# x loaded last, the last three blocks of w_ada summed on VectorE, and a new order of the Gram, index and corner steps

## The reference

```python
mod = c @ w_ada + b_ada                       # c (1, 1024), w_ada (1024, 3072)
shift, scale, gate = split(mod, 3)
h = rmsnorm(x, pre_norm_gain) * (1 + scale) + shift
proj = h @ w_in                               # 10,328 columns
# branch A: an indexer picks 128 keys per query, then softmax attention
logits = einsum('bqhd,bsd->bqhs', rope(q_idx), rope(k_idx)) * 64 ** -0.5
score = einsum('bqh,bqhs->bqs', w_idx, relu(logits)) * 8 ** -0.5
# branch B: gated delta rule in chunks, 8 heads
lower = where(strict, einsum(kb, kc) * decay, 0)   # the Gram product of the keys
t_mat = inverse(lower + eye)
u, w = t_mat @ vb, t_mat @ (kb * exp(gc)); then a scan over the chunks
y = sigmoid(ga) * y_a + sigmoid(gb) * y_b
out = x + gate * rmsnorm(y @ w_o, post_norm_gain)
```

## Time and profile before

| | |
|---|---|
| median of 3 runs | 853.12 us (852.45 to 854.57) |
| profiled execution | 849.76 us, its span 848.0 us, mean TensorE clock 0.989 |
| TensorE matmuls busy | 812.6 us, 96% |
| VectorE / GpSimd / ScalarE busy | 439.2 / 394.3 / 332.2 us |
| moved by DMA | 95.63 MB |

### The profile page before, as it was taken

One profiled execution on the slowest core, in us unless ns is written; L12 is line 12 of the kernel. 1 busy time (PEld: TensorE's weight loads), 2 busy tenths in 40 slices (PEclk: granted clock), 3 DMA queues, 4 the chain that ended last, 5 costly groups with the idle time before them and its releaser, 6 DMA issues.

```text
span 848.0 us, 11222 instructions
## 1 busy us (share of the span) xinstructions
PE 812.6 (96%) x4070; PEld 653.4 (77%) x4070; DVE 439.2 (52%) x953; ACT 332.2 (39%) x702; POOL 394.3 (46%) x335
## 2 busy tenths in 40 slices
...
GB/s 311 344 58 145 142 187 184 110 106 100 69 118 93 91 92 102 74 102 82 81 58 92 51 75 74 76 75 75 74 75 75 75 174 125 196 151 75 199 27 100
DMA packets 166801, 95.63 MB, mean 113 GB/s; under 512 B 35009, under 2 KB 158274, under 8 KB 165722
## 3 DMA queue, kind: packets, MB, share of 16 engines
...
...
## 4 chain that ended last, share of the span: by engine, by line
PE 73%; DVE 11%; DMA 5%; ACT 4%; SPq 3%; issue 2%; POOL 1%; POOLq 0%; DVEq 0%; ACTq 0%
PE ps L685 17%; PE ps L687 17%; PE ps L686 16%; PE ps L956 2%; PE ps L1007 2%; PE ps L1006 2%; PE ps L1005 2%; DMA w_ada_sb<-in_w_ada 2%; PE ps L943 2%; PE ps L796 2%; PE ps L724 2%; ACT prob L1258 2%; DVE kraw L1699 1%; DVE prob L1879 1%; PE ps L950 1%
## 5 line engine op out<-in xcount | busy, mean ns | idle before, releaser
L1356 POOL TENSOR_TENSOR w_lo<-raw,w_hi 128x512 fp32r<-128x512 f32 (+1 forms) x218 | 297.4, 1387 | 327.0 <-ACT w_hi L1029 310.8
L685 PE MATMUL ps<-h_hi,w_hi 128*128 128x512 f32 (+1 forms) x680 | 291.3, 428 | 3.2 <-ACT xT L1051 1.1
L687 PE MATMUL ps<-h_hi,w_lo 128*128 128x512 f32 (+1 forms) x680 | 268.0, 394 | 0.0
L686 PE MATMUL ps<-h_lo,w_hi 128*128 128x512 f32 (+1 forms) x680 | 266.9, 393 | 0.0
L685 PEld LDWEIGHTS ps<-h_hi,w_hi 128*128 128x128 f32 (+1 forms) x680 | 128.9, 190 | 30.3 <-issue 5.0
L687 PEld LDWEIGHTS ps<-h_hi,w_lo 128*128 128x128 f32 (+1 forms) x680 | 128.3, 189 | 29.3
L686 PEld LDWEIGHTS ps<-h_lo,w_hi 128*128 128x128 f32 (+1 forms) x680 | 129.1, 190 | 25.2 <-issue 3.4
L1029 ACT ACTIVATE w_hi<-raw 128x1024 fp32r<-128x1024 f32 (+1 forms) x109 | 113.6, 1051 | 25.9 <-PE ps L1007 17.1
L1198 ACT ACTIVATE o_tok<-ps 128x128 f32<-128x128 f32 x32 | 8.9, 277 | 91.8 <-PE ps L908 91.7
L1006 PE MATMUL ps<-w_lo,y_hi 128*128 128x256 f32 x128 | 36.2, 283 | 0.0
L1007 PE MATMUL ps<-w_hi,y_lo 128*128 128x256 f32 x128 | 36.2, 283 | 0.0
...
## 6 DMA issues: line engine op xcount, KB each, us to landing
...
```

Source lines behind the costliest of these rows:

```text
L685: pe.matmul(out_ap, w_hi[:, slot, k, 0:m], rhs_hi(k), start=(k == 0), stop=False)
L686: pe.matmul(out_ap, w_hi[:, slot, k, 0:m], rhs_lo(k), start=False, stop=False)
L687: mm = pe.matmul(out_ap, w_lo[:, slot, k, 0:m], rhs_hi(k), start=False, stop=(k == KT - 1))
L1356: ins = pool.tensor_tensor(w_lo[:, slot, ks, 0:n], raw[:, slot, ks, 0:n], w_hi[:, slot, ks, 0:n].bitcast(F32), ALU.subtract)
```

## The change

Seven edits, all in the first third of the program:

- SyncE issues all eight w_ada blocks before x.
- TensorE multiplies blocks 0 to 4 as before. VectorE forms c5 * block 5 + c6 * block 6 + c7 * block 7 in place of block 5, and TensorE multiplies this with a matrix of ones. Three filler products follow.
- ScalarE makes the sine tables before the squares; GpSimd makes a root per x tile; VectorE scales tiles 0 and 1 before mod and tiles 2 and 3 behind the first `scales`.
- w_lo of unit 2 is made by VectorE behind the last h_lo, and GpSimd goes on with unit 3.
- Gram products 0 to 3 get a bank each (5, 4, 6, 7) and come one round earlier; Gram 5, 6 and 7 come later.
- The rotation of the index rows comes one round earlier on GpSimd and VectorE; they go back in two halves, the second behind the store of the inverse; ScalarE takes the index steps ahead of the key steps within a round.
- The first four heads' corners end at round 51 instead of 53, and the zeroing moves from rounds 22, 26, 40, 43 to 2, 10, 46, 50.

```diff
-R_GRAM = [12, 13, 14, 17, R_DELTA[0] + 1, R_DELTA[0] + 4, R_DELTA[0] + 7, R_DELTA[1] + 6]
+R_GRAM = [11, 12, 13, 16, R_DELTA[0] + 1, R_DELTA[0] + 6, R_DELTA[1] + 3, R_DELTA[1] + 7]
-R_PAIR = [[42, 44, 45, 47, 49, 50, 52, 53], ...
+R_PAIR = [[41, 42, 44, 45, 47, 48, 50, 51], ...
-    GRAM_BANK = [5, 4, 5, 4, 5, 5, 5, 5]
+    GRAM_BANK = [5, 4, 6, 7, 5, 5, 5, 5]
 # SyncE
-        conditioning(2)
-        conditioning(3)
+        for k in range(2, KT):
+            conditioning(k)
         for i in range(NT):
             sp.dma_start(x_sb[:, i, :], x[blk(i), :]).then_inc(s_x[i], 16)
-        for k in range(4, KT):
-            conditioning(k)
...
-            if r == R_TURN + 3:
-                index_rows_back()
+            if r == R_TURN + 2:
+                index_rows_back((0, 1))
...
                 if r == R_STORE[b]:
                     store_inverse(b)
+                    if b == 0:
+                        index_rows_back((2, 3))
...
-            if r in (22, 26, 40, 43):
-                clear(((22, 26, 40, 43).index(r),))
+            if r in (2, 10, 46, 50):
+                clear(((2, 10, 46, 50).index(r),))
 # TensorE
-        condition(range(2, KT)).then_inc(*pro_pe.inc("mod"))
+        condition(range(2, K_VEC))
+        pe.wait_ge(*pro_pool.at("ones"))
+        pe.wait_ge(*pro_dve.at(f"acc{KT - 1}"))
+        for n in range(4):
+            mm = pe.matmul(bank(2 + n), ones_p[:], w_ada_sb[:, K_VEC, n * S:(n + 1) * S], start=False, stop=True)
+        mm.then_inc(*pro_pe.inc("mod"))
+        for _ in range(3):
+            pe.matmul(bank(0), cb[:, KT - 1, :], w_ada_sb[:, KT - 1, 0:S], start=True, stop=True)
...
         def gram(h):
             pe.wait_ge(*key_dve.at("s", h))
-            if h >= 2:
-                pe.wait_ge(*gram_dve.at("L", h - 2 if h < 4 else h - 1))
+            if h == 2:
+                pe.wait_ge(*small_dve.at("gc"))
+                pe.wait_ge(*small_act.at("gcT"))
             if h >= 4:
-                pe.wait_ge(*solve_act.at("kd", h // 7))
+                pe.wait_ge(*gram_dve.at("L", h - 1))
+                pe.wait_ge(*solve_act.at("kd", h // 6))
 # ScalarE: the three sines move ahead of the four squares; index_rows(r) moves ahead of small(r)
 # GpSimd
+            pool.tensor_scalar(small_cols[:, 4 + i:5 + i], small_cols[:, i:i + 1], 1.0 / D, EPS, ALU.mult, ALU.add)...
+            pool.tensor_tensor(small_cols[:, 4 + i:5 + i], small_cols[:, 4 + i:5 + i], nhalf[:, 0:1], ALU.pow)...
-        pool.wait_ge(*pro_dve.at("lo7"))
-        for q in range(2, RING):
-            split(q)
+        pool.wait_ge(lo_made, 3)
+        split(3)
-            if r == R_TURN + 1:
+            if r == R_TURN:
                 index_rows()
 # VectorE
+        acc = w_ada_sb[:, K_VEC, :]
+        for k in range(K_VEC, KT):
+            c_col = pcol[:, 0, R_C + k:R_C + k + 1]
+            dve.wait_ge(s_ada[k], 16)
+            if k == K_VEC:
+                dve.tensor_scalar(acc, acc, c_col, None, ALU.mult)...
+            else:
+                dve.scalar_tensor_tensor(out=acc, in0=w_ada_sb[:, k, :], scalar=c_col, in1=acc, op0=ALU.mult, op1=ALU.add)...
...
+        scale_rows(0)
+        scale_rows(1)
         dve.wait_ge(*pro_pe.at("mod"))
...
         scales(0)
+        scale_rows(2)
+        scale_rows(3)
...
+        dve.tensor_tensor(w_lo[:, 2], raw[:, 2], w_hi[:, 2].bitcast(F32), ALU.subtract).then_inc(lo_made, 1)
```

More of the change, by code:

```diff
@@ L53 @@
 RING = 4
+K_VEC = 5
 PROJ_BANKS = 3
@@ L87 @@
 R_STORE = [R_INV[b] + len(INV_ROWS[b]) for b in range(2)]
-R_PAIR = [[42, 44, 45, 47, 49, 50, 52, 53], [R_DELTA[2] + n for n in (12, 14, 16, 18, 20, 24, 26, 27)]]
+R_PAIR = [[41, 42, 44, 45, 47, 48, 50, 51], [R_DELTA[2] + n for n in (12, 14, 16, 18, 20, 24, 26, 27)]]
 R_LOAD = [max(R_DELTA[h] - 2, R_PAIR[h // 4][-1] + 3) for h in range(HEADS)]
@@ L176, in program @@
     nhalf = place("nhalf", [P, 8])
+    ones_p = place("ones_p", [P, P])
     m8 = place("m8", [P, 3, 8])
@@ L364, in program @@
     pro_pe = steps("pro_pe", ["rowsT", "rows2T", "mod"] + [f"x{k}" for k in range(KT)])
-    pro_act = steps("pro_act", [f"ssq{i}" for i in range(NT)] + ["sinA", "sinI", "cos"]
+    pro_act = steps("pro_act", ["sinA", "sinI", "cos"] + [f"ssq{i}" for i in range(NT)]
                     + [f"{a}{k}" for n in range(0, KT, 2) for a, k in (("hi", n), ("h", n + 1), ("hi", n + 1))])
@@ L368, in program @@
                                 "wrap", "rc2", "clamp", "clampc", "pcol2", "hgain"]
-                    + [f"xn{i}" for i in range(NT)] + [f"{a}{k}" for k in range(4) for a in ("shift", "scale")] + ["mb0", "scg0"]
+                    + [f"acc{k}" for k in range(K_VEC, KT)] + ["xn0", "xn1"]
+                    + [f"{a}{k}" for k in range(4) for a in ("shift", "scale")] + ["mb0", "scg0", "xn2", "xn3"]
                     + ["h0", "lo0", "shift4", "scale4", "lo1", "shift5", "scale5", "h2", "lo2", "shift6", "scale6", "lo3",
                        "shift7", "scale7", "mb1", "scg1", "h4", "lo4", "lo5", "h6", "lo6", "lo7"])
-    pro_pool = steps("pro_pool", ["half", "ms", "rstd", "kpadE", "kpadO", "zero"])
+    pro_pool = steps("pro_pool", ["half", "ones"] + [f"{a}{i}" for i in range(NT) for a in ("ms", "rstd")] + ["kpadE", "kpadO", "zero"])
     small_pe = steps("small_pe", ["smT", "gc", "gl", "gcT", "kT"])
@@ L592, in index_rows, with index_rows_back @@
                 sp.dma_start(isw[32 * n + 16 * b:32 * n + 16 * b + 16, 0, :], iq[64 * b:64 * b + 16, n, :]).then_inc(s_turned, 16)
-        def index_rows_back():
+        def index_rows_back(pairs):
             sp.wait_ge(*iq_dve.at("ad"))
-            for n in range(4):
+            for n in pairs:
                 for b in range(2):
@@ L723, in condition @@
                 for n in range(4):
-                    mm = pe.matmul(bank(2 + n), cb[:, k, :], w_ada_sb[:, k, n * S:(n + 1) * S], start=(k == 0),
-                                   stop=(k == KT - 1))
-            return mm
+                    pe.matmul(bank(2 + n), cb[:, k, :], w_ada_sb[:, k, n * S:(n + 1) * S], start=(k == 0), stop=False)
         pe.wait_ge(*pro_dve.at("cb"))
@@ L1029, in split @@
             act.activation(w_hi[:, slot, :, 0:n], raw[:, slot, :, 0:n], ACT.Copy).then_inc(hi_made, 1)
+        act.wait_ge(s_cols, 16)
+        act.wait_ge(*pro_dve.at("clampc"))
+        for t, name in ((0, "sinA"), (1, "sinI")):
+            act.activation(tab_sin[:, t, :], rp[:, 2, t * S:(t + 1) * S], ACT.Sin, scale=cols[:, 2 + t:3 + t]).then_inc(
+                *pro_act.inc(name))
+        act.activation(tab_cos[:].rearrange("p a b -> p (a b)"), rp[:, 3, :], ACT.Sin).then_inc(*pro_act.inc("cos"))
         for i in range(NT):
@@ L1311, in _ @@
                 attend(h, r - R_ATT[h])
+            index_rows(r)
             small(r)
@@ L1325, in _ @@
                     up_decay(h)
-            index_rows(r)
             for n in range(KT):
@@ L1360, in _ @@
         pool.memset(nhalf[:], -0.5).then_inc(*pro_pool.inc("half"))
+        pool.memset(ones_p[:], 1.0).then_inc(*pro_pool.inc("ones"))
         pool.wait_ge(*pro_pool.at("half"))
```

32 lines of the change are left out of this document (16 added, 16 removed).

## The result

The changed kernel takes 831.75 us (median of 4 runs, 830.45 to 832.78) against 853.48 for the kernel before (4 runs, 852.45 to 854.57): a ratio of 0.974, with a 95% interval of 0.972 to 0.977, so 21.7 us less. The forecast was 839.0, with a range of 829 to 849. The direction and the range held; the gain was 7.6 us larger than forecast.

The account below looks back on a forecast made before the run. TensorE, busy 812.6 of 848.0 us, was taken as the bound, with its waits and slow clock to win. Terms 3.5 + 0 + 7.0 + 7.4 - 1.3 - 2.5 = 14.1 us, so 853.1 - 14.1 = 839.0, range 829 to 849.

Parts of the forecast that it names:

- prologue: Before the rounds: h of tile 0 starts at 37.9 to 38.0 against 41.5, 3.5 us won (1.8 to 3.8).
- Grams and index rows, by round 39: Up to round 39: earlier L of head 3 and index rows, less a new relu wait, win 7.0 us (4.0 to 11.2).
- corners, U, Gram 5: Around 160 to 200 us: earlier corners and U, later Gram 5; 7.4 us won after Gram 6's 1.0 (3.0 to 9.6).
- Gram 6 in head 0's scan: Round 71: Gram 6's 2.4 us on VectorE stand before a state update; 1.3 us lost (0 to 3).
- new slow-clock losses: New waits in prologue, at relu and Zs: one and a half charged at 1.7 us, 2.5 us lost (0 to 5).
- w_lo of unit 2: Rounds 0 to 6: the 1.0 us wait for w_lo goes, but TensorE then waits for g; gain 0 (0 to 0.3).
- TensorE itself gains only 0.3: Gram products 0 to 3: wait of 2.6 replaced by 2.4 for K3's swish, clock loss again; 0.3 us won (0.3 to 4.3).
- TensorE waits there about 2 us: Logit products by round 39: with index rows back in time, ScalarE's first relu, ending near 126.7, is late; about 2 us wait.
- VectorE as the bound: Rival for the middle rounds: VectorE becomes the bound, only half of 7.0 and 7.4 is kept; 845 us, chance 0.20.
- All waits vanish, no clock is lost: Rival for the middle stretch: every wait goes, no clock lost anew; 23.7 us won, 829 us, chance 0.12.
- The transfers landed in the order issued: Prologue rival claimed the opposite: transfers finish together, h starts 3.1 us later than now; 846 us, chance 0.05.
- Slower through the scan of head 0: Rival for rounds 70 to 80: six products each wait behind Grams on VectorE and lose clock; 860 us, chance 0.05.

Follow-up runs that it names:

- m_con: Changed kernel with GpSimd's w_lo of units 0 and 1 held back until VectorE has made h_lo of tile 0; 837.69 us in one run.
- u_gram: Changed kernel with Gram products 0 to 3 put back in banks 5, 4, 5, 4 and rounds 12, 13, 14, 17; 833.21 us, ratio to before 0.978.
- u_index: Changed kernel with index rows' rotation a round later, return undivided, ScalarE's old order and zeroing at rounds 22, 26, 40, 43; 841.52 us, ratio to before 0.988.
- m_swish: Changed kernel with K3's swish on VectorE two rounds earlier, between Gram 1 and Gram 2; 831.22 us, ratio to before 0.976.
- u_pro: Changed kernel with its prologue put back, including w_lo of unit 2 on GpSimd, all edits of the rounds kept; 838.16 us, ratio to before 0.982.
- best: Changed kernel with K3's swish earlier, x tiles 2 and 3 scaled on ScalarE, g's last steps before K0's swish, Gram 5 a round later; 826.96 us, ratio 0.972.
- m_fill: Changed kernel with two useless float32 products on TensorE in the wait ahead of Gram 3; 831.28 us, ratio to before 0.977.
- u_corner: Changed kernel with first corners back at rounds 42 to 53 and Gram products 5, 6, 7 at rounds 56, 59, 74; 839.58 us, ratio to before 0.986.

## Why the prediction came out as it did

Against the profiled executions, 17.0 us in all, the terms read as follows.

| term | forecast | found |
|---|---|---|
| prologue | 3.5 | 2.2 at g |
| Grams and index rows, by round 39 | 7.0 | 9.7 - 2.2 = 7.5 |
| corners, U, Gram 5 | 7.4 | 19.3 - 9.7 - 1.0 = 8.6 |
| Gram 6 in head 0's scan | -1.3 | -1.3 (all that is given back behind Z32) |
| new slow-clock losses | -2.5 | 0 |
| sum | 14.1 | 17.0 |

So the mechanism, read on the two traces, came out 2.9 us larger than forecast. The other 4.7 of the 7.6 us are not in any term (see below).

**Prologue.** The steps up to mod were right: extraction at 33.70 (forecast near 33.7), a wait of 1.6 ahead of the ones product (1.8). What failed is "2 x 0.69" for the late row scalings and, behind it, the pace of the h chain: they took 2.09 us, h began at 38.75 instead of 38.0, and h_lo of tile 0 took 1.54. (The recorded terms, 37.2 and half of 1.04, give 37.7 and not 38.0; the transposes between took 0.75.) m_con shows the cause, GpSimd's subtractions of w_lo beside them. In the kernel before these scalings lay ahead of mod (25.44 to 28.18), where GpSimd was idle; the step moved into its way. The Trainium skill, SBUF: State Buffer, section "Who interferes with whom", says that a VectorE instruction with two inputs in SBUF contends with a GpSimd instruction that reads SBUF, that one in a two-port mode contends too, and that others do not. The trace agrees for h_lo, which has two SBUF inputs (1.54 against 0.69), and for the step at 38.75, which reads PSUM beside the same subtractions and kept its 0.81. The scalings have one SBUF input; whether they ran in a two-port mode no trace here says, only that they slowed.

**w_lo of unit 2.** Taken at 0, and right: the wait for w_lo is gone and one of 1.27 for g is there (forecast 1.0).

**Grams.** "TensorE itself gains only 0.3", with a new wait of 2.4 for K3's swish: 2.49 was found, and u_gram shows one wait in the other's place. The forecast also let all that hangs on L of head 3 start 3.9 earlier, and its lower bound of 4.0 stood on that. u_gram takes it away, and its profiled execution stands 0.6 behind at logit product 2 and at the product behind Z32, and not at all at the end. u_index stands 5.6 behind at logit product 2 (129.51 against 123.91). So most of the 7.5 is owed to the edits of the index rows, little to the Grams alone, and 1.3 shows in neither.

**Index rows.** The rows were back in time, as forecast. "TensorE waits there about 2 us" for the relu failed: it was 0.24. The relu itself was placed well (126.7, less 2.2 is 124.5; found just ahead of 123.91), but TensorE was not: "1 us or so earlier" at logit product 0 should have been the 0.2 that it gains at the Grams (its old place, 123.4, less the prologue's 2.2 is 121.2; found 121.03). In m_swish, where TensorE does come 3.9 earlier, the relu costs 1.8.

**Corners and U.** Each step came true once the 9.7 us won ahead are taken off: last corner forecast 169.8, so 160.1, found 159.5; U there when TensorE comes (178.7, so 169.0, found 168.46). L of head 4 was ready at 165.4 where 176.3 - 9.7 = 166.6 was forecast, and VectorE stayed 1.2 ahead: product behind Z32 185.0, so 175.3, found 174.05. That is the 1.2 by which the term was too small.

**Slow clock.** This is the term that failed most. I charged one and a half of three new waits at 1.7 us. In the profiled execution none of the waits (1.6 and 1.8 in the prologue, 0.24 at the relu, 1.81 at Zs) brought it. So what the rule of the Trainium skill (TensorE: Matmul & The Clock Gate, section "HAM oscillation") would give, 834.8, was 4.2 nearer. But 1.7 of that 4.2 was for Gram 3, where the trace does not agree with the rule: its gap of 2.49 was followed by a clock of 0.50 from 90 to 92. And the rest was luck in part: over the fourteen profiled executions of this case, TensorE's gaps between 58 and 300 us, and what the clock did in the 4 us behind them, were (0.50 is 1.2 GHz)

| gap, us | gaps | clock fell to 0.50 |
|---|---|---|
| 1.2 to 1.7 | 26 | 0 |
| 1.78 to 1.99 | 10 | 3 |
| 2.36 to 2.92 | 12 | 10 |
| 3.05 and more | 6 | 6 |

Two gaps of 1.81 at the same place, in the changed kernel and in u_pro, came out differently. The prologue's gaps between 24 and 58 us, left out of the table, brought the slow clock less often: none of seven of 1.48 to 1.75, one of thirteen of 1.78 to 1.87 (in m_con), and none of four of 2.11 to 2.78 (best, m_fill, u_index, u_gram). One more, of 2.03 in m_con, came with the clock at 0.50 already. By these counts, which were not known then, a gap of 1.8 is worth a charge of 0.2 to 0.3 times 1.7, and one of 1.3 to 1.7 nothing. The forecast's 1.7 for "a wait of 2.6 us or more" was in turn too low for the longest: behind the gaps of 4.17 (before) and 4.49 (u_corner) TensorE worked another 5 us or more at 0.50, so 2.5 us or more were lost.

**From the profile to the median.** The remaining 4.7 us (21.7 against 17.0) are not in any term. I took the profiled execution's distance to the median, 3.4, as fixed and subtracted the same 14.1 from both. It isn't fixed: before's profiled execution lies 3.7 below the median of its runs (853.48), and the changed kernel's lies 1.0 above that of its own (831.75); together that is the 4.7. Why before's was so fast is open, as its mean clock (0.989) was that of its other runs (0.987 to 0.993) and only one execution of each kernel has a trace. It is also not shown that fewer long waits make the runs agree better. In the four runs each of the result before's spread over 2.1 us and the changed kernel's over 2.3; u_corner, with gaps of 2.6, 3.1 and 4.5, spread over 2.0, and m_swish, whose profile has none above 1.82 behind 20 us, over 6.7. Nor is all of the spread the clock: two runs of u_pro at a mean clock of 0.997 and 0.998 took 837.01 and 833.77.

**Rivals.** VectorE as the bound (845): it is late at every new wait, but this rival kept only half of 7.0 and 7.4, and 7.5 and 8.6 were found. "All waits vanish, no clock is lost" (829) missed the median by only 2.8 us, but that is luck: it asked for 23.7 us, the two traces show 17.0, and the rest of its nearness is the 4.7 just named. Its condition failed too, with 2.5 us and a clock loss left at Gram 3 and 1.8 at Zs. The transfers landed in the order issued: VectorE started on block 5 at 22.5 and on block 6 at 25.0 (forecast 22.7 and 25.2). Slower through the scan of head 0: no wait there is above 1.3.
